# Weights, input and down projection stored as one contiguous piece per partition, the modulation units in another order

## The chip, the cores and the metric

The kernel runs on one core of one Trainium2 chip. The metric is the device time in microseconds (us) of one execution; lower is better. Three executions of the kernel before took 1996.77, 1990.82 and 1996.61 us, a median of 1996.61 us.

## The reference

The program is two networks in a row on 512 tokens of width 1024, all in float32. The first is a block with adaptive modulation, differential attention beside a pooling branch, and a mixture of experts:

```python
mod = silu(c) @ w_ada + b_ada                    # 1024 -> 6 x 1024: sh1, sc1, g1, sh2, sc2, g2
h = rms_norm(x, norm1_g) * (1 + sc1) + sh1
z = h @ w_in                                     # 1024 x 2048: q, k, v, u
mix = concat(diff_attention(q, k, v), pool(u)) @ w_out
x = x + g1 * mix
h = rms_norm(x, norm2_g) * (1 + sc2) + sh2
y = sum over the 2 chosen of 32 experts: (silu(h @ w_gate[e]) * (h @ w_up[e])) @ w_down[e]
x = x + g2 * y
```

Each expert has three matrices of 2 MB: w_gate and w_up (1024 x 512) and w_down (512 x 1024). The second network has two layers; each projects the normed x by w_in_2 (1024 x 3448), runs a gated delta net, a latent attention and an RWKV branch on the result, and projects back by w_out_2 (1024 x 1024).

## The kernel before, in words

Every product is made on TensorE (PE) in float32. The five engines run their own instruction streams and meet by semaphores; `take` (line 92) waits for a semaphore and clears it.

**Units and slots.** Weights come in units of 1024 rows by 512 columns (2 MB). A unit lies in SBUF as 8 row groups of 128 partitions, so a partition holds 8 x 2 KB. SyncE (SP) issues one DMA per unit into a ring of 6 slots of 16 KB per partition (line 1891), in the order of the list `units`: four units of w_ada (shift 0 and 1, scale 2 and 3), then four times one unit of w_in and two of w_ada, then two of w_out, 18 in all. A DMA waits only until its slot's last user has released it. In HBM the arrays have the reference's layout, so a unit is read in 1024 pieces of 2 KB, one per row.

**The start.** ScalarE (ACT) issues three small loads first: parameters p1, the first columns of the constants c_sb, and the broadcast row r1. Their common semaphore `params_loaded` holds back ACT, VectorE (DVE) and PE. SP issues x and the first units at the same time. PE sums the squares of x (line 2040), multiplies silu(c) by the four w_ada units (`mod_products`, line 2057, two PSUM banks in turn), ACT copies each row of results out (`mod_moved`, line 2357), and PE turns it into columns in bank 7 (`mod_columns`, line 2067). DVE waits for all four units, adds the bias (line 2581), makes the gains (lines 2587, 2588) and scales the 8 tiles of x (line 2593); ACT adds the shift to each (line 2374), and PE starts the input projection (line 2091) tile by tile. Between `mod_moved` and these 8 tiles ACT issues four side loads (lines 2367 to 2370): the late constants (cosines and sines), w_pool, and the two router matrices, the last two in pieces of 16 and 128 bytes.

**Behind it.** PE runs through 16 column tiles of the projection (lines 2091, 2103, 2115) with small `mod_columns` between them. DVE rotates q and k (lines 2616 to 2618, from the late constants), computes the other eight w_ada products itself (`mod_unit`, lines 2604 and 2606), and then pools (lines 2629 to 2635), for which GpSimd (POOL) loads the reciprocal counts (line 1941). Attention, the output projection and routing follow.

**The experts.** 32 experts are worked one after the other. SP loads each as three units into 8 slots (line 1897), in a ring too. w_gate and w_up are read as 128 pieces of 16 KB (partition p holds rows 8p to 8p+7), w_down as 256 pieces of 8 KB (two row blocks of 256, two rows a partition in each). PE multiplies gate and up (line 2253) and down (line 2269); POOL gathers the tokens' rows and scatters the results by indirect DMA (lines 1973, 1986).

**The second network** loads w_in_2 in eight units of 256 to 512 columns and w_out_2 in two, into two slots in turn (line 458), in pieces of 1 to 2 KB.

Of the kernel before, what the change touches and what calls it, by code (L numbers as in the profile page):

```python
# [17 lines left out]
ALU = mybir.AluOpType  # L18
# [3 lines left out]
P = 128  # L22
T = 512
D = 1024
# [52 lines left out]
C_DECAY = float(np.exp(-0.5))  # L77

UNITS2 = [(1024, 384), (1408, 504), (1912, 384), (2552, 512), (3064, 384), (2296, 256), (0, 512), (512, 512)]
P2 = {}  # L80
N_P2 = _cols(P2, [("next_g", 8), ("conv", 45), ("gdn_g", 1), ("qn_g", 2), ("kvn_g", 1), ("mu0", 7), ("mu1", 7),
                  ("k_k", 2), ("k_a", 2), ("r_k", 2), ("ln_g", 2), ("ln_b", 2), ("w0", 4), ("a0", 4)])
# [49 lines left out]
        self.n = 0  # L132


def build(nc, xT_d, zero_row, par1, row1, cn, invcnt, w_ada, w_in, w_pool, w_out, w_rg, w_re, w_gate, w_up, w_down,
          w2, out):
    ctx = ExitStack()
    with ctx:
# [170 lines left out]


        def ada_unit(n):
            return w_ada[0, :, n * 512:(n + 1) * 512].rearrange("(k p) n -> p k n", p=P)
        def in_unit(n):
            return w_in[0, :, n * 512:(n + 1) * 512].rearrange("(k p) n -> p k n", p=P)
        def out_unit(n):
            return w_out[0, :, n * 512:(n + 1) * 512].rearrange("(k p) n -> p k n", p=P)
        units = [ada_unit(n) for n in range(4)]
        ada_at, in_at = list(range(4)), []
        for n in range(4):
            in_at.append(len(units))  # L320
            ada_at += [len(units) + 1, len(units) + 2]
# [6 lines left out]
        def slot(n, k=8):  # L328
            return ring[:, n % SLOTS, :].rearrange("p (k n) -> p k n", k=k)
# [122 lines left out]
        def sp_second(sp):  # L452
            for l in range(LAYERS):
                def unit(n):
                    take(sp, slot_free[n % 2])
                    src, c, w = (w_in2, *UNITS2[n]) if n < 8 else (w_out2, 512 * (n - 8), 512)
                    src = src[bass.ds(l, 1), :, c:c + w].rearrange("a (k p) n -> p (a k) n", p=P)
                    sp.dma_start(slot2(n), src).then_inc(slot_full[n % 2], 16)
# [1426 lines left out]

        @block.sync
        def _(sp):
            sp.dma_start(xT[:], xT_d.rearrange("(k p) t -> p k t", p=P)).then_inc(sem("x_loaded"), 16)
            for n, u in enumerate(units):
                take(sp, slot_free[n % SLOTS])  # L1890
                sp.dma_start(slot(n), u).then_inc(slot_full[n % SLOTS], 16)
            sp.dma_start(y_d, zero_row.to_broadcast([2 * T, D])).then_inc(sem("y_loaded"), 16)
            def weights_unit(e, i, s):
                w, c = ((w_gate, 1), (w_up, 1), (w_down, 2))[i]
                take(sp, slot_free[s])
                src = w[0, bass.ds(e, 1)].rearrange("a (c p k) n -> p (a c) (k n)", c=c, p=P)
                sp.dma_start(e_slot(s, c), src).then_inc(slot_full[s], 16)
            with sp.Fori(0, N_EXP // 8) as group:
                for n in range(8):
                    for i in range(3):  # L1900
# [132 lines left out]
        def _(pe):  # L2033
# [26 lines left out]
            def mod_columns(u):  # L2060

                take(pe, sem(f"wT_full{u % 2}"))
                if u % 4 == 0:
                    take(pe, bank_free[7])
                for m in range(4):
                    col = 4 * (u % 4) + m
                    mm = pe.matmul(bank[7][:, col:col + 1], mod_rows[:, u % 2, m * P:(m + 1) * P],
                                   quarters if u < 4 else ones[:, 0:1], start=True, stop=True)
                if u % 4 == 3:
                    mm.then_inc(for_dve[7], 1)  # L2070
                elif u >= 4:
                    mm.then_inc(sem(f"wT_free{u % 2}"), 1)

            sumsq(1, KD, 0)
            for u in range(4):
                mod_products(u)
                if u > 0:
                    mod_columns(u - 1)
            mod_columns(3)

            for n in range(2):
                s = in_at[n] % SLOTS
# [244 lines left out]
        def _(act):  # L2327
# [34 lines left out]
            act.wait_ge(sem("x_loaded"), 16)  # L2362
            squares(lambda i: xT[:, i, :], KD)
            inverse_root(1, 1.0 / D)
            for u in range(4):
                mod_moved(u)
            act.dma_start(c_sb[:, late_cols:], cn[:, late_cols:]).then_inc(sem("pool_w_loaded"), 16)
            act.dma_start(pool_w[:], w_pool[0].rearrange("g c d -> c g d")).then_inc(sem("pool_w_loaded"), 16)
            act.dma_start(w_router[:, :, 0:4], w_rg[0].rearrange("(k p) n -> p k n", p=P)).then_inc(sem("router_loaded"), 16)
            act.dma_start(w_router[:, :, 4:36], w_re[0].rearrange("(k p) n -> p k n", p=P)).then_inc(sem("router_loaded"), 16)  # L2370
            act.wait_ge(sem("mod_ready"), 1)
            for k in range(KD):
                act.wait_ge(sem("scaled"), k + 1)
                act.activation(hT[:, k, :], hT[:, k, :], ACT.Identity, bias=mod[:, k:k + 1]).then_inc(sem("h_ready"), 1)  # L2374
            for i in range(8):
                b = 2 + i % 2
                take(act, for_act[b])
# [187 lines left out]
        def _(dve):  # L2565
# [12 lines left out]
            def modulation(first, b):  # L2578
                take(dve, for_dve[b])
                c0 = first  # L2580
                chain(dve.tensor_tensor(mod[:, c0:c0 + 16], bank[b][:, 0:16], par("b_ada", c0, 16), ALU.add))
                dve.sem_inc(bank_free[b], 1)
                dve.sem_inc(sem("mod_ready"), 1)

# [5 lines left out]
            def normed(which, n):  # L2590
                dve.wait_ge(sem("rs_ready"), n)
                for k in range(KD):
                    dve.scalar_tensor_tensor(hT[:, k, :], xT[:, k, :], gs[:, which, k:k + 1], rs[:],
                                             ALU.mult, ALU.mult).then_inc(sem("scaled"), 1)

            def mod_unit(u):
# [9 lines left out]
                        chain(dve.scalar_tensor_tensor(row, w, small[:, k:k + 1], row, ALU.mult, ALU.add))  # L2606
                dve.sem_inc(slot_free[s], 1)
                dve.sem_inc(sem(f"wT_full{u % 2}"), 1)
            modulation(0, 7)
            gains(0, par("norm1_g", 0, 8))  # L2610
            normed(0, 1)
            for i in range(8):
                dve.wait_ge(sem("raw_ready"), i + 1)
                if i == 0:
# [29 lines left out]
            dve.wait_ge(sem("router_loaded"), 32)  # L2644
# [373 lines left out]
    return c  # L3018


def second_inputs(a, put):

    def col(v, n):
# [5 lines left out]
    for l in range(LAYERS):  # L3029
# [17 lines left out]
    pair = np.arange(MH)[:, None] * P  # L3047
    ukv_cols = np.concatenate([(pair + np.arange(64)[None]).reshape(-1), (pair + 64 + np.arange(64)[None]).reshape(-1)])
    w = {n: put(n + "_2", np.asarray(a[n + "_2"])[..., order]) for n, order in
         (("w_in", w_in_cols), ("mla_w_uq", uq_cols), ("mla_w_ukv", ukv_cols))}  # L3050
    w.update({n: put(n + "_2", a[n + "_2"]) for n in ("w_out", "rwkv_w2", "rwkv_a2", "positions")})
# [30 lines left out]
```

## Time and profile before

| | us |
|---|---|
| three runs | 1996.77, 1990.82, 1996.61 (median 1996.61) |
| span of the profiled execution | 2001.2 |
| PE busy | 1764.2 (88%) |
| DVE, ACT, POOL busy | 857.6, 592.7, 243.5 |
| DMA | 307.75 MB, mean 154 GB/s |

The span of the profiled execution is the only time that it has; it runs from the first to the last instruction. Times in rows count from its start. The page cuts the span into 40 slices of 50 us. DMA packets are the pieces that one of the 16 DMA engines moves at a time. Queue q1 is SP's, q10 is ACT's, q0 is POOL's.

### The profile page before, as it was taken

Reading aid. Unit: us, or ns where it says so; the run is one execution under the profiler, and the core shown is the slowest. Engines: PE = TensorE matmul, PEld = TensorE weight load, DVE = VectorE, ACT = ScalarE, POOL = GpSimd, SP = SyncE. Lnnn points to the kernel's source line nnn. Section 1 sums busy time; section 2 is a strip of 40 time slices with the busy share of each in tenths; the row PEclk is TensorE's granted clock in tenths of the full one; section 3 lists DMA queues with packets and bytes.
Section 4 is the critical chain, followed back from the end, with each engine's and each line's share of the span. In section 5 each row is a group of like instructions: output and inputs, shape, how many; then the busy total and the mean of one; then the engine's idle time right before and its main releaser. Section 6 shows DMA issues by size and latency. Waiting matters only on the chain.

```text
span 2001.2 us, 44027 instructions
## 1 busy us (share of the span) xinstructions
PE 1764.2 (88%) x17970; PEld 1033.3 (52%) x17970; DVE 857.6 (43%) x1514; ACT 592.7 (30%) x1018; POOL 243.5 (12%) x270
## 2 busy tenths in 40 slices
PE   5998895977778877898999899999989998899996
PEld 2444543544444444445865784354447856853452
DVE  1567524111111111367666753151457747642331
ACT  3314521000000000334324424252253325424442
POOL 0002211111111111006112100001002103000001
PEclk8998996999999999998999999999999999999998
DMA  9758025999999999521000003110211000012101
GB/s 358 259 197 291 1 69 220 370 423 424 423 424 424 425 424 413 216 74 33 3 3 2 3 20 109 42 43 32 80 43 35 3 2 2 4 65 104 42 1 42
DMA packets 75098, 307.75 MB, mean 154 GB/s; under 512 B 10908, under 2 KB 22300, under 8 KB 57888
## 3 DMA queue, kind: packets, MB, share of 16 engines
q1 hardware_dynamic: 63280, 291.98, 37.2%
q0 software_dynamic: 5360, 9.33, 1.3%
q10 hardware_dynamic: 6272, 3.81, 0.6%
q8 instruction: 135, 2.21, 0.5%
q14 instruction: 51, 0.42, 0.1%
HBM read 301.01 MB, written 16.52 MB: 159 GB/s over the span
## 4 chain that ended last, share of the span: by engine, by line
PE 73%; DVE 13%; another core or an unknown queue 6%; ACT 4%; issue 3%; DMA 1%; DVEq 0%; ACTq 0%; POOL 0%; POOLq 0%
PE bank L2253 12%; PE bank L496 12%; PE bank L2269 6%; PE bank L1027 6%; PE bank L525 5%; PE bank L532 4%; PE bank L2091 3%; PE bank L2175 3%; PE bank L998 2%; DVE arena L1596 2%; ACT arena L1039 1%; PE bank L512 1%; PE bank L2115 1%; PE bank L2103 1%
## 5 line engine op out<-in xcount | busy, mean ns | idle before, releaser
L496 PE MATMUL bank<-hT,arena 128*128 128x512 f32 (+1 forms) x640 | 287.7, 605 | 3.6 <-ACTq L1040 2.4
L2253 PE MATMUL bank<-arena 128*64 128x256 f32 x1792 | 216.3, 399 | 66.9 <-remote 66.9
L525 PE MATMUL bank<-arena 64*64 64x64 f32 x6656 | 215.5, 220 | 22.7 <-DVE arena L1726 7.2
L525 PEld LDWEIGHTS bank<-arena 64*64 64x64 f32 x6656 | 203.8, 136 | 37.0 <-DVE arena L1726 10.1
L2253 PEld LDWEIGHTS bank<-arena 128*64 128x64 f32 x1792 | 135.6, 143 | 158.0 <-issue 107.8
L496 PEld LDWEIGHTS bank<-hT,arena 128*128 128x128 f32 (+1 forms) x640 | 122.9, 194 | 161.2 <-issue 156.6
L2859 DVE COPY arena<-bank 128x256 f32<-128x256 f32 x32 | 13.6, 425 | 329.6 <-PE bank L2261 329.6
L2269 PE MATMUL bank<-arena 128*64 128x512 f32 x448 | 104.0, 606 | 16.4 <-remote 16.4
L1027 PE MATMUL bank<-arena 128*128 128x512 f32 x256 | 110.4, 593 | 0.0
L1039 ACT ACTIVATE arena<-bank 128x512 f32<-128x512 f32 (+2 forms) x124 | 73.2, 590 | 118.9 <-PE bank L496 79.2
L532 PE MATMUL bank<-hT,arena 128*128 128x512 f32 x224 | 105.0, 607 | 1.7 <-remote 1.7
L2513 ACT ACTIVATE arena<-bank 128x512 f32<-128x512 f32 x32 | 19.1, 597 | 292.8 <-PE bank L2269 292.8
L1027 PEld LDWEIGHTS bank<-arena 128*128 128x128 f32 x256 | 48.5, 190 | 60.6 <-issue 60.1
L1852 DVE TENSOR_REDUCE arena<-bank 128x1 f32<-128x512 f32 x48 | 33.2, 692 | 106.0 <-PE bank L998 104.7
L2506 ACT ACTIVATE arena<-bank 128x256 f32<-128x256 f32 x32 | 12.3, 383 | 187.7 <-remote 187.7
L2269 PEld LDWEIGHTS bank<-arena 128*64 128x64 f32 x448 | 31.0, 138 | 69.7 <-issue 69.7
L512 PE MATMUL bank<-c_sb,arena 128*128 128x128 f32 x352 | 54.1, 288 | 12.8 <-ACTq L1040 7.9
L2091 PE MATMUL bank<-hT,arena 128*128 128x512 f32 x128 | 58.6, 619 | 5.3 <-ACT hT L2374 5.3
L532 PEld LDWEIGHTS bank<-hT,arena 128*128 128x128 f32 x224 | 39.8, 189 | 42.9 <-issue 41.2
L1986 POOL DMA_INDIRECT y_scratch<-arena x31 | 31.7, 1024 | 226.6 <-remote 205.9
L1176 ACT ACTIVATE arena<-bank 128x512 f32<-128x512 f32 x60 | 35.4, 597 | 80.2 <-PE bank L525 78.4
L512 PEld LDWEIGHTS bank<-c_sb,arena 128*128 128x128 f32 x352 | 40.4, 145 | 36.2 <-issue 36.0
(448 smaller groups left out, 2677.1 us busy)
## 6 DMA issues: line engine op xcount, KB each, us to landing
arena<-w_gate SPq DMA_DIRECT2D x28, 2048.0 KB, 30.6
arena<-w_up SPq DMA_DIRECT2D x28, 2048.0 KB, 21.0
arena<-w_down SPq DMA_DIRECT2D x28, 2048.0 KB, 26.2
arena<-w_ada SPq DMA_DIRECT2D x12, 2048.0 KB, 19.7
arena<-w_in SPq DMA_DIRECT2D x10, 2048.0 KB, 11.7
arena<-w_out SPq DMA_DIRECT2D x6, 2048.0 KB, 7.6
arena<-w_in SPq DMA_DIRECT2D x6, 1536.0 KB, 6.9
hT<-w_up SPq DMA_DIRECT2D x4, 2048.0 KB, 20.9
```

The costliest lines, as they stand in the source:

```text
L496: m = pe.matmul(bank[b][0:w, :], slot2(n)[:, k, c:c + w], hT[:, k, :], start=(k == 0), stop=(k == KD - 1))
L512: m = pe.transpose(bank[b][:, ts(t)], src[:, ts(t)], ident)
L525: m = pe.matmul(o[half(f), s, t], lhs[half(f), s, t], rhs[half(f), s, t], start=True, stop=True)
L532: m = pe.matmul(bank[b][:, :], slot2(3 + PLACE[i] // 4)[:, k, (PLACE[i] % 4) * P:(PLACE[i] % 4 + 1) * P], hT[:, k, :], start=(k == 0), sto ...
L998: pe.matmul(bank[i % 4][:, :], m_q[0:QK_M, h, ts(q)], m_k[0:QK_M, h, :], start=True, stop=True).then_inc(for_dve[i % 4], 1)
L1027: m = pe.matmul(bank[b][:, :], slot2(n)[:, k, (m_ % 4) * P:(m_ % 4 + 1) * P], mix[:, k, :], start=(i == 0), stop=(i == KD - 1))
L1039: chain(act.activation(dst, src, func, **kw))
L1596: dve.copy_predicated(blocks(g_T[d]), merged(d, l, False), blocks(bank[2 + d])).then_inc(sem(f"g_t_full{d}"), 1)
L2091: mm = pe.matmul(bank[b][:, :], slot(s)[:, k, m * P:(m + 1) * P], hT[:, k, :], start=(k == 0), stop=(k == KD - 1))
L2175: mm = pe.matmul(bank[4 + i % 4][:, :], slot(out_at + i // 4)[:, k, (i % 4) * P:(i % 4 + 1) * P], mixT[:, k, :], start=(n == 0), stop=(n = ...
L2253: mm = pe.matmul(bank[b][c * CAP:(c + 1) * CAP, 0:FE // 2], XT[j][:, k % 4, k // 4, :], e_slot(e_at(e, i), KD)[:, k, c * (FE // 2):(c + 1) ...
L2269: mm = pe.matmul(bank[6 + j][c * CAP:(c + 1) * CAP, :], hidT[:, j, f % 2, f // 2, :], e_slot(e_at(e, 2), 4)[:, f, c * HALF:(c + 1) * HALF] ...
```

## The change

1. On the host, x, w_ada, w_in, w_out, w_in_2 and w_out_2 are stored unit by unit as SBUF holds them: for each of the 128 partitions one contiguous piece of 8 rows (16 KB for 512 columns, 12 KB for 384). Each unit's DMA then moves 128 pieces. w_down's rows are reordered so that a partition's four rows (2 x 2) are one piece of 16 KB. Every SBUF layout stays as it was.
2. The first four units come as scale 2, scale 3, shift 0, shift 1. Scale's columns go to bank 7 and shift's to bank 5; DVE makes the gains and scales four tiles when scale is there, adds the shift's bias, and scales the other four. ACT waits for both (`mod_ready` 2) before its first tile.
3. ACT's side loads stand behind its 8 tiles, and the two router loads are one, of 128 pieces of 1152 bytes.

```diff
@@ the units and their order
-            return w_ada[0, :, n * 512:(n + 1) * 512].rearrange("(k p) n -> p k n", p=P)
+            return w_ada[n]
...
-        units = [ada_unit(n) for n in range(4)]
-        ada_at, in_at = list(range(4)), []
+        units = [ada_unit(n) for n in (2, 3, 0, 1)]
+        ada_at, in_at = [2, 3, 0, 1], []
@@ SP
-            sp.dma_start(xT[:], xT_d.rearrange("(k p) t -> p k t", p=P)).then_inc(sem("x_loaded"), 16)
+            sp.dma_start(xT[:].rearrange("p k t -> p (k t)"), xT_d).then_inc(sem("x_loaded"), 16)
...
-                w, c = ((w_gate, 1), (w_up, 1), (w_down, 2))[i]
+                w = (w_gate, w_up, w_down)[i]
                 take(sp, slot_free[s])
-                src = w[0, bass.ds(e, 1)].rearrange("a (c p k) n -> p (a c) (k n)", c=c, p=P)
-                sp.dma_start(e_slot(s, c), src).then_inc(slot_full[s], 16)
+                src = w[0, bass.ds(e, 1)].rearrange("a (p k) n -> p (a k n)", p=P)
+                sp.dma_start(e_slots[s], src).then_inc(slot_full[s], 16)
@@ SP, second network
-                    src, c, w = (w_in2, *UNITS2[n]) if n < 8 else (w_out2, 512 * (n - 8), 512)
-                    src = src[bass.ds(l, 1), :, c:c + w].rearrange("a (k p) n -> p (a k) n", p=P)
+                    src, at, w = (w_in2, AT2[n], UNITS2[n][1]) if n < 8 else (w_out2, UNIT * (n - 8), 512)
+                    src = src[bass.ds(l, 1), :, at:at + KD * w].rearrange("a p n -> p (a n)")
@@ PE, mod_columns and the order of the start
+                b = 5 if u < 2 else 7
+                if u in (0, 2, 4, 8):
+                    take(pe, bank_free[b])
...
-            for u in range(4):
-                mod_products(u)
-                if u > 0:
-                    mod_columns(u - 1)
-            mod_columns(3)
+            mod_products(2)
+            mod_products(3)
+            mod_columns(2)
+            mod_products(0)
+            mod_columns(3)
+            mod_products(1)
+            mod_columns(0)
+            mod_columns(1)
@@ ACT
-            for u in range(4):
+            for u in (2, 3, 0, 1):
                 mod_moved(u)
-            act.dma_start(c_sb[:, late_cols:], cn[:, late_cols:]).then_inc(sem("pool_w_loaded"), 16)
-            act.dma_start(pool_w[:], w_pool[0].rearrange("g c d -> c g d")).then_inc(sem("pool_w_loaded"), 16)
-            act.dma_start(w_router[:, :, 0:4], ...)
-            act.dma_start(w_router[:, :, 4:36], ...)
-            act.wait_ge(sem("mod_ready"), 1)
+            act.wait_ge(sem("mod_ready"), 2)
             for k in range(KD):
                 act.wait_ge(sem("scaled"), k + 1)
                 act.activation(hT[:, k, :], hT[:, k, :], ACT.Identity, bias=mod[:, k:k + 1])
+            act.dma_start(c_sb[:, late_cols:], cn[:, late_cols:]).then_inc(sem("pool_w_loaded"), 16)
+            act.dma_start(pool_w[:], w_pool[0].rearrange("g c d -> c g d")).then_inc(sem("pool_w_loaded"), 16)
+            act.dma_start(w_router[:].rearrange("p k n -> p (k n)"), w_rt).then_inc(sem("router_loaded"), 16)
@@ DVE
-            modulation(0, 7)
+            modulation(8, 7, 8, 8)
             gains(0, par("norm1_g", 0, 8))
-            normed(0, 1)
+            normed(0, 1, 4)
+            modulation(0, 5, 0, 8)
+            normed(0, 1, KD, 4)
@@ host
+def as_held(w):
+    w = np.asarray(w)
+    lead = w.shape[:-2]
+    return np.moveaxis(w.reshape(*lead, KD, P, w.shape[-1]), -3, -2).reshape(*lead, P, -1)
+def by_units(w):
+    w = np.asarray(w)[0]
+    return np.stack([as_held(w[:, c:c + 512]) for c in range(0, w.shape[1], 512)])
+def hidden_rows(w):
+    w = np.asarray(w)
+    return w.reshape(1, N_EXP, 2, P, 2, D).swapaxes(2, 3).reshape(1, N_EXP, FE, D)
```

## Rows read from the trace of the kernel before

**Rows 1.** The chain of waits, 0 to 60 us: start, length, what.

```profile
23.26 3.57 PE bank L2057 x32
26.83 1.47 another core or an unknown queue
...
29.44 1.85 PE bank L2057 x16
31.30 0.98 PE bank L2067 x8
32.28 1.25 another core or an unknown queue
...
36.67 3.52 PE bank L2067 x16
...
44.66 0.73 ACT hT L2374
```

**Rows 2.** ACT's queue and instructions in order of time, and one load's time to landing.

```profile
39.05 5.51 ACTq L2370 DMA_DIRECT2D w_router<-w_re  x1
...
10.53 0.21 ACT L2334 ACTIVATE small<-p 128x8 f32<-128x8 f32 x1 [7.07 <-DMA r<-row]
...
pool_w<-positions ACTq DMA_DIRECT2D x1, 256.0 KB, 11.6
```

**Rows 3.** Whom PE waited for (us, times, longest), 45.4:165; then 820:2001, its longest.

```profile
PE bank L2091 <- ACT hT L2374: 5.3, 1, 5.3
...
PE bank L512 <- ACTq L1040: 7.9, 5, 3.3
```

**Rows 4.** Stretches: window, length, busy by engine, granted clock, DMA share, GB/s.

```profile
11.00:40.00 29.00, 23.68 (x112) 10.48 (x112) 0.60 (x4) 12.46 (x18) 0.00 (x0) 0.90 1.05 388
45.40:51.40 6.00, 5.96 (x7) 2.52 (x8) 1.21 (x2) 4.27 (x7) 0.00 (x0) 0.51 1.10 356
184.00:188.00 4.00, 4.00 (x22) 2.08 (x20) 3.26 (x8) 2.79 (x7) 1.56 (x1) 0.94 0.99 418
188.50:192.00 3.50, 3.03 (x21) 1.92 (x20) 2.80 (x6) 2.38 (x6) 1.78 (x2) 1.00 1.03 440
410.00:782.00 372.00, 291.53 (x2050) 158.37 (x2044) 60.25 (x123) 23.34 (x48) 57.66 (x95) 0.98 1.01 424
```

**Rows 5.** SP's DMA issues in order of time, in the experts.

```profile
438.17 0.33 SPq L1897 DMA_DIRECT2D arena<-w_up  x1
...
782.45 0.33 SPq L1897 DMA_DIRECT2D arena<-w_up  x1
```

**Rows 6.** POOL's waits in the experts (345:810): us in total, times, longest.

```profile
POOL y_scratch L1986 <- remote: 205.9, 28, 11.0
```

**Rows 7.** DMA queues (packets, MB, share of 16 engines), at 1.5:3 and at 305:311 us.

```profile
q1 hardware_dynamic: 62, 0.13, 35.2%
q10 hardware_dynamic: 144, 0.05, 26.5%
...
q1 hardware_dynamic: 135, 1.95, 78.4%
q10 hardware_dynamic: 130, 0.52, 21.2%
```

**Rows 8.** POOL, DVE and PE in order of time, with the idle time before.

```profile
111.11 2.44 POOL L1941 DMA_DIRECT2D arena<-invcnt  x4 [106.56 <-DVE arena L2618]
...
121.71 0.71 DVE L2629 TENSOR_TENSOR arena<-arena 128x527 f32<-128x527 f32 x1 [5.00 <-DMA arena<-invcnt]
...
135.53 0.71 DVE L2629 TENSOR_TENSOR arena<-arena 128x527 f32<-128x527 f32 x1 [3.65 <-ACTq L2396]
...
141.74 5.47 DVE L2606 SCALAR_TENSOR_TENSOR arena<-arena,small 128x512 f32<-128x512 f32 x7
...
148.16 0.95 PE L2067 MATMUL bank<-c_sb,arena 128*128 128x1 f32 x8
```

**Rows 9.** ACT in order of time, behind the third tile.

```profile
69.34 0.60 ACT L2381 ACTIVATE arena<-bank 128x512 f32<-128x512 f32 x1 [3.82 <-PE bank L2091]
```

More of the change, by code:

```diff
@@ L79 @@
 UNITS2 = [(1024, 384), (1408, 504), (1912, 384), (2552, 512), (3064, 384), (2296, 256), (0, 512), (512, 512)]
+AT2 = [KD * sum(w for _, w in UNITS2[:n]) for n in range(len(UNITS2))]
 P2 = {}
@@ L132, in reset, with build @@
         self.n = 0
-def build(nc, xT_d, zero_row, par1, row1, cn, invcnt, w_ada, w_in, w_pool, w_out, w_rg, w_re, w_gate, w_up, w_down,
+def build(nc, xT_d, zero_row, par1, row1, cn, invcnt, w_ada, w_in, w_pool, w_out, w_rt, w_gate, w_up, w_down,
           w2, out):
@@ L311, in ada_unit @@
         def ada_unit(n):
-            return w_ada[0, :, n * 512:(n + 1) * 512].rearrange("(k p) n -> p k n", p=P)
+            return w_ada[n]
         def in_unit(n):
-            return w_in[0, :, n * 512:(n + 1) * 512].rearrange("(k p) n -> p k n", p=P)
+            return w_in[n]
         def out_unit(n):
-            return w_out[0, :, n * 512:(n + 1) * 512].rearrange("(k p) n -> p k n", p=P)
-        units = [ada_unit(n) for n in range(4)]
-        ada_at, in_at = list(range(4)), []
+            return w_out[n]
+        units = [ada_unit(n) for n in (2, 3, 0, 1)]
+        ada_at, in_at = [2, 3, 0, 1], []
         for n in range(4):
@@ L455, in unit @@
                     take(sp, slot_free[n % 2])
-                    src, c, w = (w_in2, *UNITS2[n]) if n < 8 else (w_out2, 512 * (n - 8), 512)
-                    src = src[bass.ds(l, 1), :, c:c + w].rearrange("a (k p) n -> p (a k) n", p=P)
-                    sp.dma_start(slot2(n), src).then_inc(slot_full[n % 2], 16)
+                    src, at, w = (w_in2, AT2[n], UNITS2[n][1]) if n < 8 else (w_out2, UNIT * (n - 8), 512)
+                    src = src[bass.ds(l, 1), :, at:at + KD * w].rearrange("a p n -> p (a n)")
+                    sp.dma_start(arena[:, (n % 2) * UNIT:(n % 2) * UNIT + KD * w], src).then_inc(slot_full[n % 2], 16)
                 unit(0)
@@ L1887, in _ @@
         def _(sp):
-            sp.dma_start(xT[:], xT_d.rearrange("(k p) t -> p k t", p=P)).then_inc(sem("x_loaded"), 16)
+            sp.dma_start(xT[:].rearrange("p k t -> p (k t)"), xT_d).then_inc(sem("x_loaded"), 16)
             for n, u in enumerate(units):
                 take(sp, slot_free[n % SLOTS])
-                sp.dma_start(slot(n), u).then_inc(slot_full[n % SLOTS], 16)
+                sp.dma_start(ring[:, n % SLOTS, :], u).then_inc(slot_full[n % SLOTS], 16)
             sp.dma_start(y_d, zero_row.to_broadcast([2 * T, D])).then_inc(sem("y_loaded"), 16)
             def weights_unit(e, i, s):
-                w, c = ((w_gate, 1), (w_up, 1), (w_down, 2))[i]
+                w = (w_gate, w_up, w_down)[i]
                 take(sp, slot_free[s])
-                src = w[0, bass.ds(e, 1)].rearrange("a (c p k) n -> p (a c) (k n)", c=c, p=P)
-                sp.dma_start(e_slot(s, c), src).then_inc(slot_full[s], 16)
+                src = w[0, bass.ds(e, 1)].rearrange("a (p k) n -> p (a k n)", p=P)
+                sp.dma_start(e_slots[s], src).then_inc(slot_full[s], 16)
             with sp.Fori(0, N_EXP // 8) as group:
@@ L2062, in mod_columns @@
                 take(pe, sem(f"wT_full{u % 2}"))
-                if u % 4 == 0:
-                    take(pe, bank_free[7])
+                b = 5 if u < 2 else 7
+                if u in (0, 2, 4, 8):
+                    take(pe, bank_free[b])
                 for m in range(4):
                     col = 4 * (u % 4) + m
-                    mm = pe.matmul(bank[7][:, col:col + 1], mod_rows[:, u % 2, m * P:(m + 1) * P],
+                    mm = pe.matmul(bank[b][:, col:col + 1], mod_rows[:, u % 2, m * P:(m + 1) * P],
                                    quarters if u < 4 else ones[:, 0:1], start=True, stop=True)
-                if u % 4 == 3:
-                    mm.then_inc(for_dve[7], 1)
+                if u in (1, 3, 7, 11):
+                    mm.then_inc(for_dve[b], 1)
                 elif u >= 4:
@@ L2364, in _ @@
             inverse_root(1, 1.0 / D)
-            for u in range(4):
+            for u in (2, 3, 0, 1):
                 mod_moved(u)
-            act.dma_start(c_sb[:, late_cols:], cn[:, late_cols:]).then_inc(sem("pool_w_loaded"), 16)
-            act.dma_start(pool_w[:], w_pool[0].rearrange("g c d -> c g d")).then_inc(sem("pool_w_loaded"), 16)
-            act.dma_start(w_router[:, :, 0:4], w_rg[0].rearrange("(k p) n -> p k n", p=P)).then_inc(sem("router_loaded"), 16)
-            act.dma_start(w_router[:, :, 4:36], w_re[0].rearrange("(k p) n -> p k n", p=P)).then_inc(sem("router_loaded"), 16)
-            act.wait_ge(sem("mod_ready"), 1)
+            act.wait_ge(sem("mod_ready"), 2)
             for k in range(KD):
@@ L2576, in _, with modulation @@
             chain(dve.tensor_scalar(subln, par("subln_g"), 0.8, None, ALU.mult))
-            def modulation(first, b):
+            def modulation(first, b, at=0, n=16):
                 take(dve, for_dve[b])
                 c0 = first
-                chain(dve.tensor_tensor(mod[:, c0:c0 + 16], bank[b][:, 0:16], par("b_ada", c0, 16), ALU.add))
+                chain(dve.tensor_tensor(mod[:, c0:c0 + n], bank[b][:, at:at + n], par("b_ada", c0, n), ALU.add))
                 dve.sem_inc(bank_free[b], 1)
@@ L2588, in gains, with normed @@
                 chain(dve.tensor_tensor(gs[:, which, :], gs[:, which, :], g, ALU.mult))
-            def normed(which, n):
+            def normed(which, n, hi, lo=0):
                 dve.wait_ge(sem("rs_ready"), n)
-                for k in range(KD):
+                for k in range(lo, hi):
                     dve.scalar_tensor_tensor(hT[:, k, :], xT[:, k, :], gs[:, which, k:k + 1], rs[:],
@@ L2643, in _ @@
             gains(1, par("norm2_g", 0, 8))
-            dve.wait_ge(sem("router_loaded"), 32)
+            dve.wait_ge(sem("router_loaded"), 16)
             def over_cols(v):
@@ L3049, in second_inputs @@
     w = {n: put(n + "_2", np.asarray(a[n + "_2"])[..., order]) for n, order in
-         (("w_in", w_in_cols), ("mla_w_uq", uq_cols), ("mla_w_ukv", ukv_cols))}
-    w.update({n: put(n + "_2", a[n + "_2"]) for n in ("w_out", "rwkv_w2", "rwkv_a2", "positions")})
+         (("mla_w_uq", uq_cols), ("mla_w_ukv", ukv_cols))}
+    w_in = np.asarray(a["w_in_2"])[..., w_in_cols]
+    w["w_in"] = put("w_in_2", np.concatenate([as_held(w_in[..., c:c + n]) for c, n in UNITS2], axis=-1))
+    w.update({n: put(n + "_2", a[n + "_2"]) for n in ("rwkv_w2", "rwkv_a2", "positions")})
+    w["w_out"] = put("w_out_2", np.concatenate([as_held(np.asarray(a["w_out_2"])[..., c:c + 512]) for c in (0, 512)], axis=-1))
     w["par"] = put("par2", np.stack(par))
@@ L3076 @@
     out = nc.dram_tensor("out", (D, T), F32, kind="ExternalOutput").ap()
-    build(nc, put("xT_in", np.asarray(x)[0].T), put("zero_row", np.zeros((1, D), np.float32)), put("par1", par1), put("row1", row1), put("cn", cn), put("invcnt", ic),
-          put("w_ada", w_ada), put("w_in", np.asarray(w_in)[..., rotary_columns()]), put("w_pool", w_pool), put("w_out", w_out), put("w_rg", w_router_group),
-          put("w_re", w_router_expert), put("w_gate", w_gate), put("w_up", w_up), put("w_down", w_down), second_inputs({**rest, "final_norm_g_2": final_norm_g_2}, put), out)
+    build(nc, put("xT_in", as_held(np.asarray(x)[0].T)), put("zero_row", np.zeros((1, D), np.float32)), put("par1", par1), put("row1", row1), put("cn", cn), put("invcnt", ic),
+          put("w_ada", by_units(w_ada)), put("w_in", by_units(np.asarray(w_in)[..., rotary_columns()])), put("w_pool", w_pool), put("w_out", by_units(w_out)),
+          put("w_rt", as_held(np.concatenate([np.asarray(w_router_group)[0], np.asarray(w_router_expert)[0]], axis=1))),
+          put("w_gate", w_gate), put("w_up", w_up), put("w_down", hidden_rows(w_down)), second_inputs({**rest, "final_norm_g_2": final_norm_g_2}, put), out)
     r = run_bass_kernel_spmd(nc, [arrays], core_ids=[0])
```

## The prediction, made before the change was run

> **What bounds the kernel now.** I read the chain of waits first. At the start it runs through PE and two stops: the fourth w_ada unit, for which PE stands 1.25 us, and ACT, whose first tile begins at 44.66, 4.5 us after the last column product (36.67 + 3.52 = 40.19) [rows 1]. ACT's queue says why: the issue of the second router load takes 5.51 us from 39.05, to 44.56, so ACT could not come sooner [rows 2]. PE starts the input projection at 44.66 + 0.73 + 0.05 = 45.44, its one wait until 165 us [rows 3]; what moves that start moves all behind it.
>
> Then the stretches. From 410 to 782 us the 16 DMA engines are full (share 1.01, 424 GB/s) while PE is busy 291.5 of 372 us [rows 4]: the experts go at the pace of the weights. Between SP's issues of w_up at 438.17 and 782.45 lie 22 experts, 15.65 us each [rows 5]. The same rows show 2 KB pieces at 388 GB/s under a share of 1.05, so 388/1.05 = 369 GB/s of full engines.
>
> Last, PE's waits from 820 us on: the longest is for ACT, and none is for a DMA [rows 3].
>
> **The change part by part.** I price everything against the profiled execution (span 2001.2 us) and take the difference off the median 1996.61, 4.6 us below that span.
>
> *Pieces of 16 KB, experts.* w_gate and w_up are in such pieces already; only w_down changes, from 8 KB. At 184:188 (pieces of 8 KB) full engines move 418/0.99 = 422 GB/s, at 188.5:192 (16 KB but for six) 440/1.03 = 427 [rows 4]. 2.097 MB take 4.97 and 4.91 us; with the shares' third digit (0.995) it is 4.99, so 0.08 us a unit. Full engines last from about 372 us to the landing of expert 30's w_up near 788, so (788 - 372)/15.65 = 27 units: 27 x 0.08 = 2.2 us less. Bounds: nothing, if the bytes alone set the pace, and 27 x 0.25 = 6.8 us by the bare rates 440 and 418. I take 2.2, since the share is full in both rows. POOL's indirect DMAs wait behind larger pieces, but POOL stands 205.9/28 = 7.4 us per expert for others [rows 6]; that hides about four packets of 0.3 us.
>
> *The order at the start.* Count from S, the end of the sums of squares (23.26). Now PE starts the projection 22.2 us after S. In the new order PE makes two products (3.57), waits for ACT's two tables and its first copy (1.47 and 0.09, as now), makes columns (0.98), a product (1.85), columns, a product, columns, columns: 3.57 + 1.56 + 4 x 0.98 + 2 x 1.85 = 12.75 [rows 1]. DVE's gains and its first four tiles lie beside the last two products and columns; the shift's bias takes about 0.4, ACT's first tile 0.78: 13.9 us. The wait for a DMA goes (with 4.91 us a unit the fourth lands near 28.5, needed 9 us behind S), ACT's wait in its own issues goes, and so does what the half clock took of the last product and columns (3.52 for two). That is 22.2 - 13.9 = 8.3 us less. The first tile's first seven matmuls ran at a granted clock of 0.51, which is the 1.2 GHz level, in 5.96 us, 0.43 each more than at full clock [rows 4], 3.0 us in all. Ahead of them PE did only one-column products and stood 5.3 us. The new order also puts one-column products and a short stand ahead of them, so I leave the 3.0 us where they are. Bounds: 3.0 us less, or 2.0 more if the half clock takes the last two columns too.
>
> *Small loads beside big pieces.* This speaks against the change. ACT's three first loads put 8 packets each on every engine. `params_loaded` comes at 10.53 us [rows 2], and ACT, DVE and PE all stand for it. When two queues have work they pass about equal numbers of packets: at 305:311, 135 of q1 (16 KB) beside 130 of q10 [rows 7]. So each small packet costs a big one's time: now 2.097 MB/1024 x 16 / 369 GB/s = 0.089 us, then 0.614. The first load slips ahead of x (144 small packets to 62 by 3 us [rows 7]). The other two, 16 packets an engine, start near 4 us and take 16 x (0.614 + 0.08) = 11.1: all there near 15.5 instead of 10.5, **5.0 us more**. Bounds: nothing, if they pass before x's pieces take the engines; and 13.1 more by the one load that stood beside 16 KB pieces, which took 11.6 us for 8 packets an engine [rows 2], so 6.1 us ahead of its 8 x 0.69: 0.74 + 6.1 + 24 x 0.70 = 23.6. I take 5.0, as nearly nothing is queued at the very start. x itself is then early and hidden by this.
>
> *A rule beside it.* The Trainium skill ("DMA: Bandwidth & Descriptors", Queues, rings and completion order) says that an engine takes turns by whole packets of typically 9 to 17 descriptors. The trace agrees on equal shares but cannot show the grain of a turn; I keep its result for a rival.
>
> *POOL's counts.* The load of line 1941 (1 MB in pieces of 4 KB, 16 an engine) is issued at 111.11, and DVE stands 5.00 us for it until 121.71 [rows 8], beside a unit of w_in and two of w_ada. Beside 16 KB pieces its packets take 16 x (0.614 + 0.16) = 12.4 us behind about 4.2 of latency and 0.6 of receipt: 17.2 instead of 10.6, **6.6 us late**. The three units' backlog (3 x 4.91 and the load's own 2.6) lasts as long. DVE makes up 3.65 us before its fourth group. PE's columns at 148.16 come 0.95 us behind DVE's row (141.74 + 5.47) [rows 8]. So PE stands 6.6 - 3.65 - 0.95 = 2.0 us. Bounds 0 and 4.
>
> *At nothing.* The late constants and w_pool are issued some 5 us later and land near 61 us, when SP's backlog (x and ten units, 11 x 4.91, and the small loads) is through near 59.5. DVE must have rotated tile 0 before ACT takes the third tile, now at 69.34 [rows 9], then near 66.1; 61 + 2.1 is 3 us early. If w_pool still stood beside big pieces, each microsecond over 3 would be PE's. The router load comes at one go 100 us ahead of its use. The second network's units land sooner, but PE waits for none [rows 3].
>
> The sum: -8.3 + 5.0 + 2.0 - 2.2 = -3.5 us. The profiled execution would be 1997.7, the median **1993.1 us**.
>
> **The rivals.**
> 1. *The small loads aren't late.* For: the first load's packets go well ahead of x, and 128 pieces may be described faster than 1024. Against: equal shares in [rows 7]. Then -8.5: 1988.1 us.
> 2. *Coarse turns.* The two loads' 16 packets an engine pass in one turn behind 16 big ones: near 2 + 16 x 0.614 + 1.6 = 13.4, so 2.9 late instead of 5.0: 1991.0 us. That is the skill's rule cited above.
> 3. *The clock stays up.* PE's stand ahead of the first tile shrinks from 5.3 to about 1 us. Against: columns of one element before it. Then 3.0 less: 1990.1 us.
> 4. *Slower.* Place: `params_loaded`. Each of ACT's first loads pays what the positions load paid, and the start comes 13.1 us late: -3.5 - 5.0 + 13.1 = +4.6: 2001.2 us. It decides from a landing at 10.5 + 8.5 = 19.0 us on. For: that 11.6 us row; against: its queue was full when it came.
> 5. *w_down's layout gives nothing*, since the share is already full: 1995.3 us.
>
> **How the numbers follow.** My forecast has 0.36, the rivals 0.17, 0.10, 0.15, 0.10 and 0.10, two hundredths are for none of them. The range, 1986 to 2001, leaves out pairs of gains together and most of the slower case; the likeliest one's own is 1989 to 1997 (its bounds on the counts' load and on w_down). 0.3% is 6.0 us, about what a measurement of this kernel can tell from no change: below 1990.6 lie rival 1, half of 3, and tails of 2 and of the forecast, 0.42 in all; above 2002.6 the upper part of rival 4, 0.07; between them 0.51.
>
> **What would show it.** In the changed kernel's profile: ACT's Silu near 15.5 us instead of 10.53, standing for r; 14 us from the last sum of squares to the first projection matmul, no PE stand for a DMA between them; that matmul near 42; DVE's stand for the counts' load near 11 us instead of 5.0, and PE standing 1 to 3 us for a column product near 145; the experts' issues 15.57 us apart instead of 15.65; PE's waits from 820 us on as they are. I am wrong if the Silu comes before 12 or behind 19 us, if the experts' pace moves by more than 0.25 us each, or if PE's first seven projection matmuls run at full clock.

## The result and the profile after

| | before | changed |
|---|---|---|
| median of 6 runs each, us | 1997.32 (1990.82 to 1999.12) | 2005.45 (2003.50 to 2009.85) |
| span of the profiled execution, us | 2001.2 | 2007.9 |
| DMA packets | 75098 | 34122 |
| matmuls | 17970 | 17970 |

The changed kernel takes 1.0047 of the time before [1.0031, 1.0063]: slower, by some 8 us in the medians and 6.7 us between the profiled spans. The forecast was 1993.1 us, and 2005.45 lies above its range.

The chain of waits of the changed kernel from 0 to 60 us (start, us, what), to be read against [rows 1]:

```profile
1.67 18.52 DMA r<-row
23.10 4.38 PE bank L2041 x6
...
32.69 3.57 PE bank L2058 x32
36.26 1.47 another core or an unknown queue
...
43.21 3.65 PE bank L2058 x16
...
50.18 10.08 PE bank L2096 x19
```

Before, the last of ACT's small loads took 8.8 us to land; it now takes 18.5, and PE makes its first product at 32.69 instead of 23.26. From there to the first projection matmul it takes 17.5 us instead of 22.2. The wait for the fourth unit and the stop in ACT's issues are gone, as meant, but the last product takes 3.65 us where a product of the same size took 1.85 before (at 29.44 in [rows 1]).

The timeline of the same run (start, us, what, in brackets what it stood for) at the other places, to be read against [rows 2, 5, 8]:

```profile
20.21 0.21 ACT L2339 ACTIVATE small<-p 128x8 f32<-128x8 f32 x1 [16.77 <-DMA r<-row]
...
114.59 2.44 POOL L1942 DMA_DIRECT2D arena<-invcnt  x4 [110.04 <-DVE arena L2624]
134.72 0.71 DVE L2635 TENSOR_TENSOR arena<-arena 128x527 f32<-128x527 f32 x1 [14.54 <-DMA arena<-invcnt]
151.13 5.48 DVE L2610 SCALAR_TENSOR_TENSOR arena<-arena,small 128x512 f32<-128x512 f32 x7
157.04 1.86 PE L2069 MATMUL bank<-c_sb,arena 128*128 128x1 f32 x8 [5.23 <-remote]
...
447.99 0.33 SPq L1898 DMA_DIRECT2D arena<-w_up  x1
791.04 0.33 SPq L1898 DMA_DIRECT2D arena<-w_up  x1
```

The counts' load, issued at 114.59, lets DVE go on at 134.72: 20.1 us, against 10.6 before. DVE stands 14.5 us instead of 5.0, and PE 5.2 us for the column product at 157.04. The last two rows are 22 experts apart: 343.05/22 = 15.59 us each, 15.65 before.

Three stretches (length; busy us of PE, PE's loads, DVE, ACT and POOL with instructions; granted clock; DMA share; GB/s). The first and the second lie around the two places, the third in the experts [rows 4]:

```profile
39.90:46.70 6.80, 6.80 (x32) 2.38 (x24) 2.95 (x7) 0.60 (x1) 0.00 (x0) 0.50 0.99 402
155.90:162.80 6.90, 5.76 (x13) 3.56 (x14) 6.20 (x9) 0.00 (x0) 0.00 (x0) 0.51 0.75 271
410.00:782.00 372.00, 289.84 (x2062) 157.16 (x2060) 60.27 (x123) 23.52 (x48) 58.74 (x97) 0.99 1.01 426
```

Both places ran at the 1.2 GHz level (a granted clock of 0.50 and 0.51), the second right behind PE's stand of 5.2 us. The experts' DMA moves 426 GB/s where it moved 424.

The same PE instruction in both traces gives the ledger, changed minus before, in us:

| at | difference | step |
|---|---|---|
| first product (32.69, before 23.26) | +9.4 | small loads late |
| first projection matmul | +4.7 | new order |
| projection past both half clocks | +3.5 | first tiles at half clock for a shorter time |
| behind the column product at 157.04 | +11.8 | counts late (5.2) and half clock behind them (3.1) |
| 230 us | +11.5 | |
| 360 us | +10.0 | the clock was low for longer in the trace before |
| 784 us, after 27 experts | +8.2 | w_down |
| 1261 to 1570 us (second network) | +5.6 | comes and goes, see the last section |
| end of the span | +6.7 | |

### The profile page after: what moved, and what is told of

Its sections match the earlier page's. It is cut to its first block, busy times and chain, and to the rows that moved or that the text cites. A ratio compares the mean times of both kernels' runs of the same rounds, so it can differ in the third digit from the quotient of the medians.

```text
span 2007.9 us, 44031 instructions
## 1 busy us (share of the span) xinstructions
PE 1756.4 (87%) x17970; PEld 1028.4 (51%) x17970; DVE 857.5 (43%) x1515; ACT 592.5 (30%) x1018; POOL 243.2 (12%) x270
## 2 busy tenths in 40 slices
DMA packets 34122, 307.75 MB, mean 153 GB/s; under 512 B 8844, under 2 KB 10124, under 8 KB 16016
## 4 chain that ended last, share of the span: by engine, by line
PE 73%; DVE 12%; another core or an unknown queue 6%; ACT 4%; issue 3%; DMA 1%; DVEq 0%; ACTq 0%; POOL 0%; POOLq 0%
PE bank L497 12%; PE bank L2258 12%; PE bank L2274 6%; PE bank L1028 5%; PE bank L526 5%; PE bank L533 4%; PE bank L2096 3%; PE bank L2180 3%; PE bank L999 2%; DVE arena L1597 2%; ACT arena L1040 2%; PE bank L513 2%; PE bank L2120 1%; PE bank L2108 1%
## 5 line engine op out<-in xcount | busy, mean ns | idle before, releaser
L526 PE MATMUL bank<-arena 64*64 64x64 f32 x6656 | 215.4, 220 | 22.2 <-DVE arena L1727 7.4
L513 PE MATMUL bank<-c_sb,arena 128*128 128x128 f32 x352 | 54.6, 291 | 14.1 <-ACTq L1041 9.2
L2274 PEld LDWEIGHTS bank<-arena 128*64 128x64 f32 x448 | 31.1, 138 | 70.0 <-issue 70.0
L513 PEld LDWEIGHTS bank<-c_sb,arena 128*128 128x128 f32 x352 | 41.2, 147 | 37.5 <-issue 37.3
L1177 ACT ACTIVATE arena<-bank 128x512 f32<-128x512 f32 x60 | 35.3, 597 | 79.7 <-PE bank L526 78.4
L1521 DVE SCALAR_TENSOR_TENSOR arena<-arena 128x512 f32<-128x512 f32 x72 | 56.6, 786 | 2.5
## 6 DMA issues: line engine op xcount, KB each, us to landing
arena<-w_ada SPq DMA_DIRECT2D x12, 2048.0 KB, 13.9
```

Of the source, the lines that this page charges most:

```text
L513: m = pe.transpose(bank[b][:, ts(t)], src[:, ts(t)], ident)
L526: m = pe.matmul(o[half(f), s, t], lhs[half(f), s, t], rhs[half(f), s, t], start=True, stop=True)
L1521: chain(dve.scalar_tensor_tensor(dst, x, w, dst, ALU.mult, ALU.add))
L2274: mm = pe.matmul(bank[6 + j][c * CAP:(c + 1) * CAP, :], hidT[:, j, f % 2, f // 2, :], e_slot(e_at(e, 2), 4)[:, f, c * HALF:(c + 1) * HALF] ...
```

## The experiments

Each ratio is against the kernel before, run on the same chip beside it. The theory to test: the small loads beside 16 KB pieces (9.4 us) and the counts' load beside them (8.3 us) turned the gain into a loss, each because a small packet waits out a big one. Its rivals are that the loss lies in the new order, that it is latency per load, and that it is in the second network's layout.

**e1, small loads first.** The changed kernel with the three small loads on SP, ahead of x:

```diff
+            sp.dma_start(p1[:], par1).then_inc(sem("params_loaded"), 16)
+            sp.dma_start(c_sb[:, 0:CN["cosA"][0]], cn[:, 0:CN["cosA"][0]]).then_inc(sem("params_loaded"), 16)
+            sp.dma_start(r1[:], row1.to_broadcast([P, N_R1])).then_inc(sem("params_loaded"), 16)
             sp.dma_start(xT[:].rearrange("p k t -> p (k t)"), xT_d).then_inc(sem("x_loaded"), 16)
...
-            act.dma_start(p1[:], par1).then_inc(sem("params_loaded"), 16)
...
```

> The changed kernel, with its three first small loads (parameters, first constants, row) issued by SP ahead of x instead of by ACT beside it, so that nothing of another queue stands beside them. Turns theory (each small packet waits one turn of a 16 KB packet): the small loads land near 5.5 us, x near 9.5, ACT's squares start near 10 instead of 22.3, the first projection matmul near 38 instead of 50.2; POOL's counts still hold PE for about 5 us and the half clock behind it. Span 12 us below the changed kernel's: near 1996, time near 1993.5. Rival (the bigger x pieces or the new order of the units hold the start): squares not before 18 us, time within 3 us of 2005.

Measured: 1995.69 us, 1.0010 [0.9995, 1.0025]. Its timeline:

```profile
6.65 0.21 ACT L2339 ACTIVATE small<-p 128x8 f32<-128x8 f32 x1 [4.63 <-DMA r<-row]
...
37.41 28.14 PE L2099 MATMUL bank<-hT,arena 128*128 128x512 f32 x61 [1.27 <-ACT hT L2375]
```

The small loads are there at 6.65 instead of 20.21, and the projection begins 12.8 us sooner. Of that 10.2 us are left from 65 us on: at 62 us PE stands 2.3 us for ACT, behind DVE, which waits for ACT's late side loads beside big pieces until 63.7. The counts are as late as in the changed kernel (DVE stands 14.34 us, PE 5.0). Against the changed kernel the ratio fell by 0.37%, 7.4 us, where 12 were expected. From the sums of squares' end (22.93) to this matmul lie 14.5 us at full clock: the order does what was priced (13.9) once the clock stays up.

**e2, counts early.** The counts loaded by SP behind the eighth unit, into SBUF that is unused:

```diff
+                if n == 7:
+                    for g in range(4):
+                        sp.dma_start(inv_c[:, g, :], invcnt[g:g + 1, :].to_broadcast([P, T])).then_inc(sem("inv_loaded"), 16)
...
-            for g in range(4):
-                pool.dma_start(inv_c[:, g, :], invcnt[g:g + 1, :].to_broadcast([P, T])).then_inc(sem("inv_loaded"), 16)
```

> The changed kernel, with POOL's load of the reciprocal counts moved to SP's queue behind the eighth unit, into SBUF that nothing else uses in the first network, so it shares no engine turns. Turns theory: the start stays at 20.2 and the first projection matmul at 50.2, DVE's stand of 14.5 us before pooling is gone, PE stands for no column product (5.2 us less) and keeps its clock there (3.1 us less): 8.3 us below the changed kernel, near 1997. Rival (DVE is late at that place for another reason, or PE's gain is eaten by attention): under 3 us less.

Measured: 1998.58 us, 1.0018 [0.9999, 1.0038]; the profiled span is 1997.0. Its timeline has

```profile
48.03 17.41 PE L2097 MATMUL bank<-hT,arena 128*128 128x512 f32 x36 [1.26 <-ACT hT L2376]
```

ACT still begins at 20.32. This matmul comes 2.1 us sooner than in the changed kernel, since the clock stayed at full level (14.3 us from the sums of squares to it). Past the column product the difference is 10.4 us, so 8.3 us came back at the counts: the stand and the half clock behind it, as in the ledger. The ratio fell by 0.29%, 5.8 us, less than the traces' 10.4; its interval, down to 0.9999, leaves room for both.

**e3, both edits.**

> Both edits on the changed kernel: the three small first loads on SP ahead of x, and the counts' load on SP behind the eighth unit. Turns theory: the two gains add, 12 + 8.3 = 20 us below the changed kernel, near 1985 and so some 12 us below the kernel before. Rival (one hides behind the other): the sum of the two is more than 4 us above what both give.

Measured: 1983.16 us, 0.9943 [0.9924, 0.9963], span 1984.5. The two edits take off 21 us of the changed kernel's time; by the traces it is 13.0 at the projection (37.19) and 8.3 at the counts. With both costs gone the new layout is faster than before. The edits help each other: e1's stand of 2.3 us at 62 us is gone, and DVE has the side loads at 56.3 instead of 63.7. From 50 to 54 us ACT's queue passes 514 packets beside 517 of SP's in e3, and 117 beside 116 in e1, since the counts' 4 KB pieces now stand in SP's queue at that time.

**e4, one load instead of three.** The three small tensors side by side in one of 3940 bytes per partition, still on ACT's queue beside x:

```diff
-            act.dma_start(p1[:], par1).then_inc(sem("params_loaded"), 16)
...
-            act.dma_start(c_sb[:, 0:late_cols], cn[:, 0:late_cols]).then_inc(sem("params_loaded"), 16)
-            act.dma_start(r1[:], row1.to_broadcast([P, N_R1])).then_inc(sem("params_loaded"), 16)
+            act.dma_start(first[:, 0:N_P1 + N_R1 + late_cols], par1).then_inc(sem("params_loaded"), 16)
```

> The changed kernel, with the three small first loads joined to one DMA of 128 pieces of 3940 bytes, still on ACT's queue beside x; the row is stored 128 times in HBM. The same bytes, a third of the packets: 8 per engine instead of 24. If what counts is the number of packets (one turn each beside 16 KB), the load lands 16 x 0.61 = 9.8 us sooner, near 10 us, and the time falls by about 10 us to 1995.5. If what counts is bytes or time shared evenly between the queues, the landing stays within 2 us of 20.2 and the time of 2005.

Measured: 1993.87 us, 0.9997 [0.9980, 1.0014].

```profile
10.19 0.21 ACT L2336 ACTIVATE small<-first 128x8 f32<-128x8 f32 x1 [7.71 <-DMA first<-par]
```

The same bytes (the row now stored once for each partition), in 8 packets an engine instead of 24, are there 10.0 us sooner, still beside x's 16 KB pieces. Its first packet starts at 3.0 us, as in the changed kernel (2.9), so the sooner issue isn't what helps. Sixteen packets fewer at 0.61 to 0.70 us are 9.8 to 11.2. So the price goes by packets. A theory of three latencies in a row would leave one of three as well; what speaks against it is the changed kernel's queue, shown in the next section, which kept passing packets. The counts remain late here: DVE stands 14.13 us for them. The clock fell (from 30.3 us on), and the first projection matmul came at 40.22, 17.4 us behind the sums of squares.

**e5, 2 KB pieces at the start.** The changed kernel, its order too, but x and the first network's units in 2 KB pieces as before (each unit still stands by itself in HBM):

```diff
-            return w_ada[n]
+            return w_ada[n].rearrange("(k p) n -> p k n", p=P)
...
-            sp.dma_start(xT[:].rearrange("p k t -> p (k t)"), xT_d).then_inc(sem("x_loaded"), 16)
+            sp.dma_start(xT[:], xT_d.rearrange("(k p) t -> p k t", p=P)).then_inc(sem("x_loaded"), 16)
```

> The changed kernel with x and the first network's units of w_ada, w_in and w_out in pieces of 2 KB again, as before; the new order of the units, the side loads behind the tiles, w_down in 16 KB pieces and the second network's layout stay. Turns theory: the small first loads land near 10.5 us as before, DVE stands near 5 us for the counts, PE stands for no column product; the reorder then shows alone: the first projection matmul near 38 to 41 us instead of 45.4, the time 4 to 8 us below the kernel before, near 1990. Rival (the new order itself costs, for the half clock or the shift units that come last): not below the kernel before.

Measured: 1987.88 us, 0.9957 [0.9942, 0.9972], span 1990.2.

```profile
10.57 0.21 ACT L2339 ACTIVATE small<-p 128x8 f32<-128x8 f32 x1 [7.11 <-DMA r<-row]
...
39.13 26.42 PE L2096 MATMUL bank<-hT,arena 128*128 128x512 f32 x57 [1.39 <-remote]
...
115.00 0.71 DVE L2635 TENSOR_TENSOR arena<-arena 128x527 f32<-128x527 f32 x1 [5.83 <-DMA arena<-invcnt]
```

The order stays, the queues are as they were, and both costs go by the size of SP's pieces alone: Silu at 10.57 (10.53 before), DVE's stand 5.83 (5.00 before). The projection begins 6.3 us ahead of 45.44, 15.0 behind the sums of squares (24.12), with the clock at its full level up to it.

**e6, w_down alone**, on the kernel before:

```diff
-                w, c = ((w_gate, 1), (w_up, 1), (w_down, 2))[i]
+                w, c = ((w_gate, 1), (w_up, 1), (w_down, 1))[i]
...
+    return w.reshape(1, N_EXP, 2, P, 2, D).swapaxes(2, 3).reshape(1, N_EXP, FE, D)
```

> The kernel before with w_down alone in pieces of 16 KB. My sum: 0.08 us per unit over 27 units, 2.2 us less (0.11%), an issue spacing of 15.57 us an expert instead of 15.65. Rival (bytes alone set the pace): no difference.

Measured: 1995.22 us, 0.9989 [0.9976, 1.0002], and 15.58 us between the issues of w_up per expert. The pace is there in the trace, 27 x 0.07 = 1.9 us; the time alone can't tell it from nothing.

**e7, e3 with e5's pieces.** 

> The kernel of e3 (both small loads out of the way) with x and the first network's units in pieces of 2 KB again. It asks whether large pieces bring anything at the start once nothing small stands beside them. With 2 KB the fourth w_ada unit lands near 34 us instead of 30, while PE asks for it near 32: the first projection matmul 1 to 3 us later than e3's 37.2, the time 1 to 4 us above e3's 1983.2. Rival (large pieces there are worth nothing): within 1 us of e3.

Measured: 1989.88 us, 0.9962 [0.9946, 0.9977]. PE stands 2.0 us for the fourth unit, the clock is at the lower level from 35.3 to 45.5 us, and the projection begins at 42.45, 5.3 us later than in e3. The time is 6.7 us above e3's, where 1 to 4 were expected.

**e8, the second network's layout alone**, on the kernel before:

```diff
-                    src = src[bass.ds(l, 1), :, c:c + w].rearrange("a (k p) n -> p (a k) n", p=P)
+                    src = src[bass.ds(l, 1), :, at:at + KD * w].rearrange("a p n -> p (a n)")
```

> The kernel before with the second network's units alone in pieces of 12 to 16 KB. No PE wait there was for a DMA, so my theory gives no difference, within 0.15%. Rival (the 3 us that the changed kernel made up between 830 and 1260 us come from sooner units): 3 us less.

Measured: 1998.34 us, 1.0004 [0.9993, 1.0015]. It costs nothing and brings nothing that can be told from noise. Its start has the same instructions as the kernel before's, yet the projection begins at 43.62 instead of 45.44: the clock fell at 38.9 instead of 34.3.

**e9 to e12, four versions side by side.** e9 is e3 with e4's single small load, on SP ahead of x. e10 is e3, e11 is e7 and e12 is e5, each run again.

> e3 with the three small first loads joked to one of 128 pieces of 3940 bytes, on SP ahead of x: two issues of 0.45 us fewer ahead of x, which ends the wait at the start (it lands at 11.7 in e3). Turns theory: ACT's squares start near 10.9 us instead of 11.8, the time 1 us below e3's. Rival (x's landing is set by something else): no difference.

> The kernel of e3 once more, to stand beside e11 and e12 on one chip: 12 to 15 us below the kernel before (0.6 to 0.75%).

> The kernel of e7 (small loads out of the way, first network's units in 2 KB pieces) beside e3's: if the large pieces pay at the start, by the two stands for DMAs that e7 showed (x at 13.6, the fourth unit 2.0 us) and the half clock behind them, it is 4 to 6 us above e3's. If e7's half clock was chance, 1 to 2 us.

> The kernel of e5 (new order, 2 KB pieces in the first network, small loads where they were) beside e3's: 8 us below the kernel before (0.4%) and 4 to 5 us above e3's.

| | us | ratio | projection begins |
|---|---|---|---|
| e9, one small load first | 1980.94 | 0.9924 [0.9912, 0.9937] | 34.71 |
| e10, three small loads first | 1986.78 | 0.9953 [0.9940, 0.9966] | 37.09 |
| e11, the same, 2 KB at the start | 1988.23 | 0.9963 [0.9950, 0.9977] | 41.96 |
| e12, new order, 2 KB at the start | 1987.90 | 0.9960 [0.9946, 0.9974] | 39.27 |

The timeline of e9:

```profile
4.07 0.21 ACT L2337 ACTIVATE small<-first 128x8 f32<-128x8 f32 x1 [2.05 <-DMA first<-par]
9.68 1.15 ACT L2346 ACTIVATE sq<-xT 128x512 f32<-128x512 f32 x2 [3.39 <-DMA xT<-xT_in]
...
34.71 25.57 PE L2097 MATMUL bank<-hT,arena 128*128 128x512 f32 x55 [1.27 <-ACT hT L2373]
```

e9 is the fastest version run, 0.76% or 15 us below the kernel before: the small loads are done at 4.07, and x alone sets the start. The squares begin at 9.68 instead of 12.07 in e10, 2.4 us sooner where 1 was expected, and PE stays 2 to 4 us ahead all the way to its last matmul. The interval of e9 and that of e10 just miss each other (e3's, [0.9924, 0.9963], overlaps), so that the single load brings something is likely, not sure.

e10 came out 0.47% below the kernel before, where 0.6 to 0.75 were expected, and e10, e11 and e12 can't be told apart by these times alone. The traces say more on the 16 KB pieces of the first network: e10 is 4.9 us ahead of e11 at the projection, and still 4.7 at 1110 us, in the second network; e3 was 5.3 ahead of e7 at the projection. And the 12 runs of e3 and e10 together have a median of 1985.5 us, the 14 of e7 and e11 one of 1988.6. So these pieces are likely to pay some 3 us of time. The larger part of e9's 15 us doesn't need them: e5 and e12, with 2 KB pieces and the three small loads and the counts' load where they were, are 8 us below the kernel before.

## Why the prediction was wrong

**The small loads: the step that failed first.** It was put at +5.0 (landing 15.5 us) and measured +9.7 (20.21, and +9.4 behind the sums of squares). The DMA queues of the changed kernel (packets, share of the stretch's engine time and of its length) within 4 to 5 us, then within 15 to 19 us:

```profile
q1 hardware_dynamic: 26, 0.43, 101.2%
q10 hardware_dynamic: 27, 0.01, 3.6%
...
q1 hardware_dynamic: 79, 1.29, 86.8%
q10 hardware_dynamic: 78, 0.09, 17.8%
```

q1 holds x and the units, q10 the small loads. The packets pass one for one, as the prediction said, and in every stretch from 3 to 19 us, so q10 was not without work there. What failed is where the count began. It let the first load slip by before x, as the 2 KB trace showed, leaving 16 packets an engine. With x in one packet per partition x's were there first (12 packets of q1 and none of q10 from 1 to 2 us), and all 24 packets waited. The three loads, issued by 1.67 us, landed at 8.4, 14.1 and 20.2 us, so the second and the third took 5.7 and 6.1 us for 8 packets an engine, 0.71 and 0.76 each, where 0.69 was put. The landing lies between the forecast (15.5) and rival 4 (23.6), past the point where that rival decides (19.0). Its place, `params_loaded`, was the right one; its price of 6.1 us of latency ahead of the first packet wasn't: q10's first packet started at 2.9 us. Rival 4 had 0.10, and that was too little beside an upper bound that the prediction had itself worked out.

**The counts: the step that failed next.** Put at +2.0, measured +8.3. The load came 9.5 us later than before by its own length (20.1 instead of 10.6), not 6.6: its pieces of 4 KB ran from 118.6 to 133.9 us, 0.95 us for each of the 16 an engine where 0.77 was put. After the slack of 3.65 and 0.95 that leaves 4.9, and PE stood 5.2. And PE came out of this stand at the 1.2 GHz level for 6.8 us, 3.1 us more. That second effect was in no bound: the prediction priced the clock at the start and not behind the stand which it forecast itself. e2 took both away together.

**The order at the start.** Put at -8.3, measured 22.2 - 17.5 = 4.7 less, and 1.3 more by the shorter half clock in the first tiles: 6.0. Part of the 22.2 was that one trace's clock: e6 and e8, which start as the kernel before does, take 21.1 and 20.1 us for the same stretch, so 6.0 is a high reading, by up to 2 us. Its count of instructions was right: at full clock the stretch takes 14.3 to 14.5 us in e1, e2, e3, e9 (34.71 - 20.30), where 13.9 was put. In the changed kernel and in e4 it takes 17.5 and 17.4, with the clock down from 39.9 to 46.7 and from 30.3. The bound "2.0 more if the half clock takes the last two columns" had the right kind and was 1 us short. Rival 3 (the first tile at full clock) is true of none of them: right at the projection's start the granted clock is 0.50 or 0.51 for 3.4 us in the changed kernel (50.1 to 53.5), e1 (37.5 to 40.9), e2, e3 and e9 (35.0 to 38.4). What stays up in e1, e2, e3 and e9 is the clock of the products and columns ahead of it.

**w_down.** Put at 15.57 us per expert and -2.2, measured 15.59 and -1.8 (10.0 to 8.2 in the ledger), 15.58 in e6. Rival 5 is out by the trace, not by the time.

**Coarse turns (rival 2).** With 26 packets of one queue to 27 of the other over 16 engines in one microsecond, and 79 to 78 in four, and the first load's 128 packets started 16 every 0.63 to 0.69 us from 2.93 us on, a turn is about one packet. The rule of the Trainium skill ("DMA: Bandwidth & Descriptors", Queues, rings and completion order), turns of 9 to 17 descriptors, is not what this trace shows.

**At nothing.** PE waits for no DMA in the second network, and e8 puts its layout at 0. The late constants cost nothing in the changed kernel, where the start was itself late. In e1, where it wasn't, ACT's side loads cost PE 2.3 us: that cover was thin, as the prediction said (3 us).

With the measured terms, 9.4 - 6.0 + 8.3 - 1.8 = +9.9 against a span 6.7 longer. Of the rest, 1.5 us went between 230 and 360 us. There the same PE instructions take 32.5 us in the trace before (from 306.6, granted clock 0.57) and 31.1 in the changed one (from 318.0, 0.64). Another 1.5 went in the second network, where the trace before has a granted clock of 0.66 from 1242 to 1247 us and the changed one 1.00 from 1248 to 1253; e6 and e8 have no fall there either. Both are differences of the clock between two single traces; that the change brought them is not shown.

## What to carry to other kernels

When the pieces of one queue grow, count the packets of every small load that runs beside it: each costs about one big packet's time, so 24 packets an engine cost, as an estimate, 24 x 0.61 = 14.6 us beside 16 KB pieces. Here the last load landed 18.5 us after its issue beside 16 KB pieces and 8.8 beside 2 KB. Put small loads that something waits for ahead on the same queue and join them into as few packets as possible; here that, with the counts' load moved too, turned a kernel 0.5% slower into one 0.8% faster. And price a stand of PE with the clock behind it, since 5.2 us of waiting cost 8.3 here. And before the larger pieces are called the gain, run the rest without them: here the rest brought over half.

## What the runs showed of the hardware

Where q1's pieces are the larger ones, two queues share the engines by packets, one for one: within 15 to 19 us q1's 79 packets took 1.29 MB and q10's 78 took 0.09 MB in the changed kernel; in e3, from 50 to 54 us, 517 and 514 passed, 1.26 and 0.29 MB; in the kernel before, from 48 to 52 us, 694 of q1 (1.39 MB in 2 KB pieces) and 693 of q10 (0.01 MB). Where the other queue's pieces are larger than q1's, q1 passes more: in the kernel before 580 of its packets (2 KB) went beside 319 of the counts' load (4 KB) from 114.9 to 121 us, and each queue had about half of the engines' time (51.5% and 51.6%). The equal numbers that the prediction put on every case hold for the changed kernel and not for that one.

The same PE instructions in the same order take 14.3 us in e2 and 17.5 in the changed kernel, at full and at half level of the granted clock. In e2 they begin at 33.70, in the changed kernel at 32.62, behind the same sums of squares; in e1 and e4 at 22.93 and 22.81. So the length of the wait ahead of them doesn't settle it, and what does stays open. Behind PE's later stand for a column product, of 5.2 us in the changed kernel, 5.0 in e1 and 4.8 in e4, the clock was at its lower level for 6.8 us each time (e1: 146.8 to 153.6, granted 0.50); behind e1's stand of 2.3 us at 62 us it stayed up (1.00 from 62 to 76). In the second network the difference between the traces of the kernel before and the changed one moves by 3.1 and by 1.4 us at two places where one has the clock down and the other hasn't (granted 0.53 from 901 to 912 us before and 0.84 from 910 to 921 in the changed kernel, and the place near 1245 us); a few microseconds between two profiles of this kernel mean nothing until the clock of both has been looked at.
